# One operand buffer in rows of 512 columns instead of 544, high and low part side by side, in all phases but the small convolution

## The chip, the core and the metric

The kernel runs on one core of one Trainium2 chip. The metric is the device time of one execution in microseconds. All data are float32 in HBM, and so is the result.

## The reference, cut to what matters

Two blocks work one after the other on x with 256 tokens of width 2048. Nearly all of the arithmetic is products of a 256-token activation with weights of 2048 rows.

```python
def first_block(...):
    h = rms_norm(r, g_mix)
    q, k, v, c_b, c_c, c_x, g_a, g_c = split(h @ w_in)           # 2048 x 10240
    attn = moba_attention(rms_norm(q), rms_norm(k), v)           # 8 heads, causal
    y_attn = attn @ w_attn_out
    y_conv = (c_b * causal_depthwise_conv(c_c * c_x, w_conv)) @ w_conv_out
    r = r + (sigmoid(g_a) * y_attn + sigmoid(g_c) * y_conv) @ w_o
    r = r + square(relu(rms_norm(r, g_mlp) @ w_up)) @ w_down     # 8192 wide
    r = r + sigmoid(rms_norm(r, g_ple) @ w_ple_gate) * (p @ w_ple_proj)

def second_block(...):
    h = concatenate([meta_tokens, x])                            # 16 + 256 tokens
    u = rms_norm(h, norm_mix_pre) @ conv_w_in + conv_b_in        # 2048 x 4096
    u = depthwise_conv_31_taps(u_a * sigmoid(u_g)) + conv_b_dw
    h = h + rms_norm(silu(layer_norm(u)) @ conv_w_out + conv_b_out, norm_mix_post)
    u = rms_norm(h, norm_ffn_pre)
    h = h + rms_norm((silu(u @ w_gate) * (u @ w_up)) @ w_down, norm_ffn_post)   # 5632 wide
    return h[:, 16:]
```

The attention of the second block is in the reference's text, but with one layer only the convolution mixer runs.

## The kernel before

**Split products.** Each float32 operand is split into a high part (rounded to `F32R`) and a low part (the rest). A product of two such operands is three products: high by high, high weight by low activation, low weight by high activation. The fourth is left out. The activation's two parts lie one behind the other in a row of one buffer, so that one matmul of 512 columns multiplies the high weight with both (line 456: `hi` by `both_parts(M, kt)`), and a second one of 256 columns multiplies the low weight with the high part (line 459, or line 465 where the low weights come late). I call the two a pair. A pair covers one inner tile `kt` (128 rows of the inner dimension, 16 of them in 2048) and one output tile `m` (128 output features).

**Two operand buffers.** `A` has 16 rows of 2 * TM = 544 columns of four bytes (line 96), since the small convolution's input has 16 meta tokens ahead of the 256. Everywhere else its high part is columns 0 to 255 and its low part columns 272 to 527, so that `both_parts(A, kt)` reads two runs of 256 columns with a gap of 16, and row `kt` begins 2176 * kt bytes behind A's start. `B` has 16 rows of 2 * T = 512 columns (line 97): the two parts touch, the read is one run of 512 columns, and row `kt` begins 2048 * kt bytes behind B's start. `part(M, ...)` (line 131) and `both_parts` (line 136) give these views.

**Which phase reads which.** `A` feeds qk, v, ga, ccx, cb, gc, w_o, down 0 to 3, conv2 (the small convolution's input product, the only phase with 272 columns, lines 745 to 747), out2, and glu 0 to 2 (the gate and up projections of the second block). `B` feeds attn_out, conv_out, up 0 to 3, gate, and back 0 to 2 (the second block's down projection, where the activation is the stationary operand and 512 weight columns move, lines 831 to 833). In v the activation from `A` is stationary too (lines 638 to 640). In out2's and glu 0's first steps two output panels go side by side (lines 495 and 497).

**Weights.** SyncE loads units of 128 x 1024 weights (four inner tiles by two output tiles, 8 pairs) into a ring of four `stage` slots. ScalarE copies each unit to `whi` (line 896), VectorE subtracts to `wlo` (line 1440; GpSimd in conv2, line 2258), TensorE uses the unit. `body` runs two steps, and a step is four units, 32 pairs, into two PSUM banks. While TensorE works on one output panel, ScalarE and VectorE empty the panel before, and where the next phase needs it they write it, split, into the buffer that TensorE isn't reading: into `A` during up, into `B` during glu.

**Order.** All waits are written out by hand with semaphores, one instruction stream per engine; nothing is scheduled by a planner. A unit's wait is at line 440 and following in `step`.

**Grouped steps.** In qk's first two bodies, ga, ccx, and cb's first (`hi_first=True`), and in the first unit of glu 1 and glu 2 (`grouped=0`), the 8 matmuls of 512 columns of a unit run first and its 8 of 256 columns after them (line 465).

Of the kernel before, what the change touches and what calls it, by code (L numbers as in the profile page):

```python
# [32 lines left out]
P = 128  # L33
# [50 lines left out]
def two_block_kernel(nc, io, out):  # L84
    at, _, UNITS = plan()

    with ExitStack() as ctx:
# [346 lines left out]
        def _(pe):  # L434
# [210 lines left out]
            body("qk", 1, A, h1, {2: [lambda: spread(0, xp[:, 0, 0:T], stat_ready)]}, hi_first=True)  # L645
            with pe.Fori(2, 4) as it:
                body("qk", it, A, h1)
            pe.wait_ge(rstd_ready, 1)
# [12 lines left out]
            v_panel(1, {4: [norms(0)]})  # L661
            body("ga", 0, A, h1, beside(0), hi_first=True)
            with pe.Fori(1, 4) as it:
                body("ga", it, A, h1, beside(it), hi_first=True)
            with pe.Fori(0, 3) as it:
                body("ccx", it, A, h1, beside(it + 4), hi_first=True)
            body("ccx", 3, A, h1, beside(7), hi_first=True)
            body("cb", 0, A, h1, beside(8), hi_first=True)
            body("cb", 1, A, h1)
            with pe.Fori(0, 4) as it:  # L670
                body("gc", it, A, h1)

# [14 lines left out]
            with pe.Fori(0, 4) as it:  # L687
                body("w_o", it, A, (merged_ready, 0, 2))

# [31 lines left out]
            ffn_panels("up0", 0, B, (r_ready, 0, 4), first_it=1)  # L721
            ffn_panels("down0", 0, A, (hidden_ready, 0, 2))
# [85 lines left out]
            keep_busy(4, gp[:, 3, :])  # L808
            side_by_side("out2", A, (ln_ready, 0))
            with pe.Fori(1, 4) as it:  # L810
                body("out2", it, A, (ln_ready, 0, 4))
            pe.wait_ge(acc_ready, 36)
# [8 lines left out]
            keep_busy(7, gp[:, 0, :])  # L821
            side_by_side("glu0", A, (r_ready, 48))
            body("glu0", 1, A, (r_ready, 48, 4), {3: [lambda: column_sums(3)]})
# [35 lines left out]
            turn_r(0)  # L859
            body("glu1", 0, A, (r_ready, 48, 4), grouped=0)  # L860
            with pe.Fori(1, 8) as it:
                body("glu1", it, A, (r_ready, 48, 4))
            with pe.Fori(0, 2) as it:
# [3 lines left out]
            turn_r(1)  # L867
            body("glu2", 0, A, (r_ready, 48, 4), grouped=0)
            with pe.Fori(1, 6) as it:
                body("glu2", it, A, (r_ready, 48, 4))  # L870
            for c in range(3):
# [18 lines left out]
        def _(act):  # L890
# [60 lines left out]
            def hi_of_x(c, half):  # L951
                act.wait_ge(x_turned, 2 * c + half + 1)
                for kk in (2 * half, 2 * half + 1):
                    nc.scalar.activation(A[:, 4 * c + kk, 0:T], x_home(c)[:, kk, :], ACT.Copy,
                                         scale=col("g_mix", 4 * c + kk)).then_inc(x_hi, 1)
# [124 lines left out]
            def conv_out_tail(hp, j):  # L1080
                for back in (1, 0) if j == 3 else (1,) if j else ():
                    act.wait_ge(merged, hp - back + 1)
                    nc.scalar.activation(part(A, 0, 2 * (hp - back), 2), s[:, (j - back) % 2, :, 0:T],
                                         ACT.Copy).then_inc(merged_hi, 1)
# [199 lines left out]
            for kt in range(2):  # L1284
                act.wait_ge(ln_normed, kt + 1)
                silu(kt, xp[:, kt, 0:T])
                act.wait_ge(ln_silu, kt + 1)
                nc.scalar.activation(part(A, 0, kt, 1), xp[:, kt, 0:T].unsqueeze(1), ACT.Copy).then_inc(ln_hi, 1)
            for c in range(1, 8):
# [5 lines left out]
                act.wait_ge(ln_silu, 2 * c + 2)  # L1295
                nc.scalar.activation(part(A, 0, 2 * c, 2), ln_home(c), ACT.Copy).then_inc(ln_hi, 2)
                if c == 3:
# [39 lines left out]
            for m in range(2):  # L1337
                act.wait_ge(first_sum, m + 1)
                nc.scalar.activation(part(A, 0, m, 1), r[:, m:m + 1, :], ACT.Copy, scale=col("ffn_pre", m)).then_inc(r_hi, 1)
            for h in range(1, 8):  # L1340
# [6 lines left out]
                act.wait_ge(post_gained, 2 * h)  # L1347
                nc.scalar.activation(part(A, 0, 2 * h, 2), gained_r(h), ACT.Copy).then_inc(r_hi, 2)
                if h == 3:
# [85 lines left out]
        def _(dve):  # L1435
# [100 lines left out]
            for c in range(4):  # L1536
                for kk in range(4):
                    kt = 4 * c + kk
                    if kt == 2:
                        dve.wait_ge(x_turned, 2)  # L1540
                        for i in (2, 3):
                            nc.vector.tensor_scalar(A[:, i, 0:T], x_home(0)[:, i, :], col("g_mix", i), None, ALU.mult).then_inc(first_made, 1)
# [4 lines left out]
                    nc.vector.scalar_tensor_tensor(A[:, kt, TM:TM + T], x_home(c)[:, kk, :], col("g_mix", kt),  # L1547
                                                   A[:, kt, 0:T].bitcast(F32), ALU.mult, ALU.subtract).then_inc(h1_ready, 1)
                take_lo(c, c)
# [172 lines left out]
            def merged_lo(h, j):  # L1722
                dve.wait_ge(merged_hi, h + 1)
                nc.vector.tensor_tensor(part(A, 1, 2 * h, 2), s[:, j, :, 0:T], part(A, 0, 2 * h, 2).bitcast(F32),
                                        ALU.subtract).then_inc(merged_ready, 1)
# [198 lines left out]
            def ln_low(kt, o):  # L1924
                n = o.shape[1]
                dve.wait_ge(ln_hi, kt + n)
                nc.vector.tensor_tensor(part(A, 1, kt, n), o, part(A, 0, kt, n).bitcast(F32), ALU.subtract).then_inc(ln_ready, n)

# [42 lines left out]
            def post_low(h):  # L1971
                dve.wait_ge(r_hi, 48 + 2 * h + 2)
                nc.vector.tensor_tensor(part(A, 1, 2 * h, 2), gained_r(h), part(A, 0, 2 * h, 2).bitcast(F32),
                                        ALU.subtract).then_inc(r_ready, 2)

            def first_low(m):
                dve.wait_ge(r_hi, 48 + m + 1)
                nc.vector.scalar_tensor_tensor(part(A, 1, m, 1), r[:, m:m + 1, :], col("ffn_pre", m),
                                               part(A, 0, m, 1).bitcast(F32), ALU.mult, ALU.subtract).then_inc(r_ready, 1)

# [426 lines left out]
```

## Time and profile before

| what | value |
|---|---|
| device time, median of 3 runs (range) | 2544.76 us (2540.75 to 2545.08) |
| the profiled execution's own time | 2541.44 us |
| its span | 2539.6 us |
| TensorE busy | 2518.6 us, 99% |
| VectorE busy | 1725.2 us, 68% |
| ScalarE busy | 1252.5 us, 49% |
| GpSimd busy | 446.3 us, 18% |
| granted TensorE clock, mean | 0.998 |
| moved by DMA | 466.46 MB, mean 184 GB/s |

The span is the profiled program from its first to its last instruction; the device time of the same execution is 1.84 us longer. Matmuls are pipelined: a row's mean of 393 ns is the time from the start of one matmul to its modelled end, and the next starts before that end. What TensorE really takes is read from start to start.

### The profile page before, as it was taken

The numbers are of one execution on the slowest core, as the hardware profiler recorded it, in microseconds if no ns is written. First come the engines' busy times: TensorE is split into PE (matmuls) and PEld (weight loads), VectorE is DVE, ScalarE is ACT, GpSimd is POOL, SyncE is SP. The second block draws the span as 40 slices with busy tenths as digits, with TensorE's granted clock in tenths as the row PEclk, the third lists the DMA queues.
The fourth block names the chain that finished last, engine by engine and source line by source line (L and its number), as shares of the span: only waits on it lengthen the run. The fifth ranks groups of instructions, "written<-read, shape, count | busy, mean of one in ns | idle before, by whom it ended". The sixth has DMA issues, their size and how long they took to land.

```text
span 2539.6 us, 42560 instructions
## 1 busy us (share of the span) xinstructions
PE 2518.6 (99%) x14597; PEld 2223.8 (88%) x14597; DVE 1725.2 (68%) x2097; ACT 1252.5 (49%) x1554; POOL 446.3 (18%) x303
## 2 busy tenths in 40 slices
PE   9999999999999999999999999999999999999998
PEld 8888888888888888888888899988888888888887
DVE  6568875587765665665667889985766556654665
ACT  6456555554544444444444554555654444444443
POOL 0034410002200000000002378973500000000001
PEclk9999999999999999999999999999999999999999
DMA  7655565665655656556565565536466656656554
GB/s 232 186 168 181 161 189 181 198 192 179 192 188 191 190 186 189 186 191 189 182 197 183 183 173 167 167 109 205 149 192 200 197 181 195 187 192 187 184 183 163
DMA packets 470966, 466.46 MB, mean 184 GB/s; under 512 B 14521, under 2 KB 441011, under 8 KB 470707
## 3 DMA queue, kind: packets, MB, share of 16 engines
q1 hardware_dynamic: 470336, 464.97, 58.6%
q8 instruction: 51, 0.84, 0.1%
q10 hardware_dynamic: 546, 0.38, 0.1%
q14 instruction: 33, 0.27, 0.0%
HBM read 463.20 MB, written 2.10 MB: 183 GB/s over the span
## 4 chain that ended last, share of the span: by engine, by line
PE 87%; DVE 9%; POOL 1%; ACT 1%; issue 1%; DMA 0%; DVEq 0%; POOLq 0%; ACTq 0%; SPq 0%
PE gp L456 48%; PE gp L459 22%; DVE xp L1856 6%; PE gp L832 3%; PE gp L831 3%; PE gp L833 3%; PE gp L465 3%; PE gp L495 1%; PE gp L638 1%; PE gp L639 1%; PE gp L640 1%; DVE wlo L1440 1%; POOL acc L2360 0%; PE xp L792 0%; DVE gp L1821 0%
## 5 line engine op out<-in xcount | busy, mean ns | idle before, releaser
L1440 DVE TENSOR_TENSOR wlo<-stage,whi 128x1024 fp32r<-128x1024 f32 x809 | 1010.0, 1263 | 671.3 <-ACT whi L896 665.9
L896 ACT ACTIVATE whi<-stage 128x1024 fp32r<-128x1024 f32 x874 | 913.5, 1057 | 919.2 <-PE gp L459 591.9
L456 PE MATMUL gp<-A,whi 128*128 128x512 f32 x3968 | 1317.4, 393 | 0.3 <-DVE A L1547 0.3
L459 PE MATMUL gp<-A,wlo 128*128 128x256 f32 x3248 | 911.0, 280 | 0.0
L456 PEld LDWEIGHTS gp<-A,whi 128*128 128x128 f32 x3968 | 738.8, 188 | 161.8 <-DVE A L1547 0.7
L459 PEld LDWEIGHTS gp<-A,wlo 128*128 128x128 f32 x3248 | 612.0, 188 | 0.0
L456 PE MATMUL gp<-B,whi 128*128 128x512 f32 x1536 | 532.9, 391 | 0.5 <-ACT work L1119 0.5
L459 PE MATMUL gp<-B,wlo 128*128 128x256 f32 x1536 | 429.3, 280 | 0.0
L456 PEld LDWEIGHTS gp<-B,whi 128*128 128x128 f32 x1536 | 287.4, 187 | 64.2 <-ACT work L1119 0.7
L459 PEld LDWEIGHTS gp<-B,wlo 128*128 128x128 f32 x1536 | 290.0, 189 | 0.0
L2161 POOL TENSOR_TENSOR sq<-r 128x512 f32 x24 | 29.5, 1227 | 791.1 <-DVE r L1750 755.5
L1856 DVE SCALAR_TENSOR_TENSOR xp<-work,taps,xp 128x256 f32<-128x256 f32 x406 | 162.9, 478 | 1.8 <-PE xp L763 1.8
L2258 POOL TENSOR_TENSOR wlo<-stage,whi 128x1024 fp32r<-128x1024 f32 x64 | 154.4, 2429 | 15.2 <-ACT whi L896 14.9
L745 PE MATMUL gp<-A,whi 128*128 128x272 f32 x512 | 150.6, 294 | 1.1 <-POOL wlo L2258 1.1
L747 PE MATMUL gp<-A,wlo 128*128 128x272 f32 x512 | 147.7, 288 | 0.0
L746 PE MATMUL gp<-A,whi 128*128 128x272 f32 x512 | 147.4, 288 | 0.0
L833 PE MATMUL gp<-whi,B 128*128 128x512 f32 (+1 forms) x352 | 135.3, 384 | 0.0
L832 PE MATMUL gp<-wlo,B 128*128 128x512 f32 (+1 forms) x352 | 135.3, 384 | 0.0
L831 PE MATMUL gp<-whi,B 128*128 128x512 f32 (+1 forms) x352 | 135.2, 384 | 0.0
L2372 POOL TENSOR_TENSOR r<-work 128x1024 f32<-128x1024 f32 (+2 forms) x6 | 10.9, 1810 | 691.1 <-DVE work L2041 684.4
L465 PEld LDWEIGHTS gp<-A,wlo 128*128 128x128 f32 x720 | 96.7, 188 | 8.5 <-DVE wlo L1440 0.4
L909 ACT ACTIVATE cross<-gp 128x512 f32<-128x512 f32 x176 | 102.4, 582 | 3.3 <-PE gp L459 3.3
(333 smaller groups left out, 2171.6 us busy)
## 6 DMA issues: line engine op xcount, KB each, us to landing
stage<-in_w_in SPq DMA_DIRECT2D x160, 512.0 KB, 4.4
stage<-in_w_up SPq DMA_DIRECT2D x128, 512.0 KB, 3.7
stage<-in_w_down SPq DMA_DIRECT2D x128, 512.0 KB, 4.5
stage<-in_ffn_w_gate SPq DMA_DIRECT2D x88, 512.0 KB, 4.5
stage<-in_ffn_w_up SPq DMA_DIRECT2D x88, 512.0 KB, 4.5
stage<-in_ffn_w_down SPq DMA_DIRECT2D x88, 512.0 KB, 4.5
stage<-in_conv_w_in SPq DMA_DIRECT2D x64, 512.0 KB, 4.0
stage<-in_w_o SPq DMA_DIRECT2D x32, 512.0 KB, 4.3
```

The lines of the kernel that those rows point to most:

```text
L456: nc.tensor.matmul(bank.rearrange("p (a t) -> p a t", a=2), hi, both_parts(M, kt), start=first, stop=False)
L459: done = nc.tensor.matmul(bank[:, T:2 * T], lo, M[:, kt, 0:T], start=False, stop=last)
L465: done = nc.tensor.matmul(gp[:, 2 * j + m, T:2 * T], wlo[:, slot, c:c + P], M[:, kt0 + 4 * u + k, 0:T], start=False, stop=u == units - 1 a ...
L745: nc.tensor.matmul(o, hi, A[:, kt, 0:TM], start=first, stop=False)
L747: done = nc.tensor.matmul(o, lo, A[:, kt, 0:TM], start=False, stop=last)
L831: nc.tensor.matmul(o, x_hi, hi[:, c:c + w], start=kt == 0, stop=False)
L832: nc.tensor.matmul(o, x_hi, lo[:, c:c + w], start=False, stop=False)
L833: return nc.tensor.matmul(o, x_lo, hi[:, c:c + w], start=False, stop=last)
L896: nc.scalar.activation(unit_homes(n, slot)[0], stage[:, slot, :], ACT.Copy).then_inc(hi_ready, 1)
L1440: nc.vector.tensor_tensor(lo, stage[:, slot, :], hi.bitcast(F32), ALU.subtract).then_inc(lo_ready, 1)
L1856: nc.vector.scalar_tensor_tensor(dst, x, w, o, ALU.mult, ALU.add).then_inc(tap_done, 1)
L2258: nc.gpsimd.tensor_tensor(wlo[:, slot, :], stage[:, slot, :], whi[:, slot, :].bitcast(F32), ALU.subtract).then_inc(lo_ready, 1)
```

## The change

A view `E` is added on the memory of `A`: its first 16 * 512 columns as 16 rows of 512. Every phase that `A` fed reads and writes `E`, except conv2 and its input, which keep `A` with its rows of 544. Since `E` isn't `A`, `part` puts its low part at column 256, and `both_parts(E, kt)` is one run of 512 columns; row `kt` begins 2048 * kt bytes behind A's start. The buffer's size, all other tensors, and the place and number of the instructions and waits on every engine are as they were. What changes is the addresses, and the shape of line 456's (and 495's) moving operand. `sums_split` for the first two norms still puts its sums in the last row of `A`, and the last two weight units still use A's first 4096 columns (`spare`).

```diff
+        E = A[:].rearrange("p k n -> p (k n)")[:, 0:KT * 2 * T].rearrange("p (k n) -> p k n", k=KT)
...
-            body("qk", 0, A, h1, hi_first=True, mid={c: lambda c=c: turn_x(c + 1) for c in range(3)})
+            body("qk", 0, E, h1, hi_first=True, mid={c: lambda c=c: turn_x(c + 1) for c in range(3)})
...
-                            x_hi, x_lo = A[:, kt, t * P:t * P + P], A[:, kt, TM + t * P:TM + t * P + P]
+                            x_hi, x_lo = E[:, kt, t * P:t * P + P], E[:, kt, T + t * P:T + t * P + P]
...
-                ffn_panels("down0", rnd, A, (hidden_ready, 8 * rnd, 2))
+                ffn_panels("down0", rnd, E, (hidden_ready, 8 * rnd, 2))
...
-            side_by_side("out2", A, (ln_ready, 0))
+            side_by_side("out2", E, (ln_ready, 0))
...
-                body("glu0", it, A, (r_ready, 48, 4))
+                body("glu0", it, E, (r_ready, 48, 4))
...
-                        nc.scalar.activation(part(A, 0, 4 * it + 2 * j, 2), s[:, j, :, 0:T], ACT.Copy).then_inc(up_hi, 1)
+                        nc.scalar.activation(part(E, 0, 4 * it + 2 * j, 2), s[:, j, :, 0:T], ACT.Copy).then_inc(up_hi, 1)
...
-                        nc.vector.tensor_tensor(part(A, 1, 4 * it + 2 * j, 2), t, part(A, 0, 4 * it + 2 * j, 2).bitcast(F32),
+                        nc.vector.tensor_tensor(part(E, 1, 4 * it + 2 * j, 2), t, part(E, 0, 4 * it + 2 * j, 2).bitcast(F32),
                                                 ALU.subtract).then_inc(hidden_ready, 1)
...
```

The other lines of the diff make the same replacement in the phases listed above.

## Rows read from the trace of the kernel before

**Rows 1.** The page: span and busy time of TensorE.
```profile
span 2539.6 us, 42560 instructions
...
PE 2518.6 (99%) x14597; PEld 2223.8 (88%) x14597; DVE 1725.2 (68%) x2097; ACT 1252.5 (49%) x1554; POOL 446.3 (18%) x303
```
**Rows 2.** The page: the chain that ended last, share of the span by engine.
```profile
PE 87%; DVE 9%; POOL 1%; ACT 1%; issue 1%; DMA 0%; DVEq 0%; POOLq 0%; ACTq 0%; SPq 0%
```
**Rows 3.** Busy time by window, down round 0, up round 1 (stretch, length, each engine, PEclk, DMA).
```profile
760.00:849.00 89.00, 89.00 (x513) 78.20 (x513) 50.69 (x51) 38.35 (x41) 0.00 (x0) 1.00 0.60 191
849.00:938.00 89.00, 89.00 (x516) 78.46 (x515) 58.86 (x63) 41.03 (x47) 0.00 (x0) 1.00 0.59 186
```
**Rows 4.** TensorE's instructions by line and form (busy us, mean ns, idle before).
```profile
L456 PE MATMUL gp<-A,whi 128*128 128x512 f32 x3968 | 1317.4, 393 | 0.3 <-DVE A L1547 0.3
L459 PE MATMUL gp<-A,wlo 128*128 128x256 f32 x3248 | 911.0, 280 | 0.0
L456 PE MATMUL gp<-B,whi 128*128 128x512 f32 x1536 | 532.9, 391 | 0.5 <-ACT work L1119 0.5
...
L465 PE MATMUL gp<-A,wlo 128*128 128x256 f32 x720 | 99.0, 280 | 0.0
L495 PE MATMUL gp<-A,whi 128*128 128x512 f32 x128 | 45.9, 401 | 1.2 <-DVE A L1927 1.2
```
**Rows 5.** Timeline, TensorE: first matmul of down 0, up 1, down 1, up 2, down 2.
```profile
760.51 0.39 PE L456 MATMUL gp<-A,whi 128*128 128x512 f32 x1
...
849.68 0.39 PE L456 MATMUL gp<-B,whi 128*128 128x512 f32 x1
...
938.42 0.39 PE L456 MATMUL gp<-A,whi 128*128 128x512 f32 x1
...
1027.60 0.39 PE L456 MATMUL gp<-B,whi 128*128 128x512 f32 x1
...
1116.34 0.39 PE L456 MATMUL gp<-A,whi 128*128 128x512 f32 x1
```
**Rows 6.** Timeline, TensorE: starts of the inner tiles 1 to 8, down round 0.
```profile
761.20 0.39 PE L456 MATMUL gp<-A,whi 128*128 128x512 f32 x1
...
761.90 0.39 PE L456 MATMUL gp<-A,whi 128*128 128x512 f32 x1
...
762.59 0.39 PE L456 MATMUL gp<-A,whi 128*128 128x512 f32 x1
...
763.29 0.39 PE L456 MATMUL gp<-A,whi 128*128 128x512 f32 x1
...
763.98 0.39 PE L456 MATMUL gp<-A,whi 128*128 128x512 f32 x1
...
764.68 0.39 PE L456 MATMUL gp<-A,whi 128*128 128x512 f32 x1
...
765.38 0.39 PE L456 MATMUL gp<-A,whi 128*128 128x512 f32 x1
...
766.08 0.39 PE L456 MATMUL gp<-A,whi 128*128 128x512 f32 x1
```
**Rows 7.** Timeline, TensorE: start of inner tile 8, up round 1.
```profile
855.22 0.39 PE L456 MATMUL gp<-B,whi 128*128 128x512 f32 x1
```
**Rows 8.** The chain that ended last: two units of grouped matmuls, four units apart.
```profile
222.20 1.85 PE gp L456 x8
...
233.35 1.85 PE gp L456 x8
```
**Rows 9.** Timeline, TensorE: wide matmuls, 18 apart, in v and in back 0.
```profile
107.26 0.39 PE L638 MATMUL gp<-whi,A 128*128 128x512 f32 x1
...
111.38 0.39 PE L638 MATMUL gp<-whi,A 128*128 128x512 f32 x1
...
1985.16 0.39 PE L831 MATMUL gp<-whi,B 128*128 128x512 f32 x1
...
1989.24 0.39 PE L831 MATMUL gp<-whi,B 128*128 128x512 f32 x1
```

More of the change, by code:

```diff
@@ L643, in v_panel @@
                         f()
-            body("qk", 1, A, h1, {2: [lambda: spread(0, xp[:, 0, 0:T], stat_ready)]}, hi_first=True)
+            body("qk", 1, E, h1, {2: [lambda: spread(0, xp[:, 0, 0:T], stat_ready)]}, hi_first=True)
             with pe.Fori(2, 4) as it:
-                body("qk", it, A, h1)
+                body("qk", it, E, h1)
             pe.wait_ge(rstd_ready, 1)
@@ L661, in _ @@
             v_panel(1, {4: [norms(0)]})
-            body("ga", 0, A, h1, beside(0), hi_first=True)
+            body("ga", 0, E, h1, beside(0), hi_first=True)
             with pe.Fori(1, 4) as it:
-                body("ga", it, A, h1, beside(it), hi_first=True)
+                body("ga", it, E, h1, beside(it), hi_first=True)
             with pe.Fori(0, 3) as it:
[L666 to L669, printed above, removed]
+                body("ccx", it, E, h1, beside(it + 4), hi_first=True)
+            body("ccx", 3, E, h1, beside(7), hi_first=True)
+            body("cb", 0, E, h1, beside(8), hi_first=True)
+            body("cb", 1, E, h1)
             with pe.Fori(0, 4) as it:
-                body("gc", it, A, h1)
+                body("gc", it, E, h1)
             for phase, kt0, ready in (("attn_out", 0, (attn_ready, HEADS, 0)), ("conv_out", CT, (conv1_ready, 0, 4))):
@@ L687, in _ @@
             with pe.Fori(0, 4) as it:
-                body("w_o", it, A, (merged_ready, 0, 2))
+                body("w_o", it, E, (merged_ready, 0, 2))
             pe.wait_ge(meta_step, 2)
@@ L821, in _ @@
             keep_busy(7, gp[:, 0, :])
-            side_by_side("glu0", A, (r_ready, 48))
-            body("glu0", 1, A, (r_ready, 48, 4), {3: [lambda: column_sums(3)]})
+            side_by_side("glu0", E, (r_ready, 48))
+            body("glu0", 1, E, (r_ready, 48, 4), {3: [lambda: column_sums(3)]})
             with pe.Fori(2, 8) as it:
-                body("glu0", it, A, (r_ready, 48, 4))
+                body("glu0", it, E, (r_ready, 48, 4))
             def products(o, n, slot, kt, k, t, a, w, last):
@@ L859, in _ @@
             turn_r(0)
-            body("glu1", 0, A, (r_ready, 48, 4), grouped=0)
+            body("glu1", 0, E, (r_ready, 48, 4), grouped=0)
             with pe.Fori(1, 8) as it:
-                body("glu1", it, A, (r_ready, 48, 4))
+                body("glu1", it, E, (r_ready, 48, 4))
             with pe.Fori(0, 2) as it:
@@ L867, in _ @@
             turn_r(1)
-            body("glu2", 0, A, (r_ready, 48, 4), grouped=0)
+            body("glu2", 0, E, (r_ready, 48, 4), grouped=0)
             with pe.Fori(1, 6) as it:
-                body("glu2", it, A, (r_ready, 48, 4))
+                body("glu2", it, E, (r_ready, 48, 4))
             for c in range(3):
@@ L1082, in conv_out_tail @@
                     act.wait_ge(merged, hp - back + 1)
-                    nc.scalar.activation(part(A, 0, 2 * (hp - back), 2), s[:, (j - back) % 2, :, 0:T],
+                    nc.scalar.activation(part(E, 0, 2 * (hp - back), 2), s[:, (j - back) % 2, :, 0:T],
                                          ACT.Copy).then_inc(merged_hi, 1)
@@ L1287, in _ @@
                 act.wait_ge(ln_silu, kt + 1)
-                nc.scalar.activation(part(A, 0, kt, 1), xp[:, kt, 0:T].unsqueeze(1), ACT.Copy).then_inc(ln_hi, 1)
+                nc.scalar.activation(part(E, 0, kt, 1), xp[:, kt, 0:T].unsqueeze(1), ACT.Copy).then_inc(ln_hi, 1)
             for c in range(1, 8):
@@ L1295, in _ @@
                 act.wait_ge(ln_silu, 2 * c + 2)
-                nc.scalar.activation(part(A, 0, 2 * c, 2), ln_home(c), ACT.Copy).then_inc(ln_hi, 2)
+                nc.scalar.activation(part(E, 0, 2 * c, 2), ln_home(c), ACT.Copy).then_inc(ln_hi, 2)
                 if c == 3:
@@ L1338, in _ @@
                 act.wait_ge(first_sum, m + 1)
-                nc.scalar.activation(part(A, 0, m, 1), r[:, m:m + 1, :], ACT.Copy, scale=col("ffn_pre", m)).then_inc(r_hi, 1)
+                nc.scalar.activation(part(E, 0, m, 1), r[:, m:m + 1, :], ACT.Copy, scale=col("ffn_pre", m)).then_inc(r_hi, 1)
             for h in range(1, 8):
@@ L1347, in _ @@
                 act.wait_ge(post_gained, 2 * h)
-                nc.scalar.activation(part(A, 0, 2 * h, 2), gained_r(h), ACT.Copy).then_inc(r_hi, 2)
+                nc.scalar.activation(part(E, 0, 2 * h, 2), gained_r(h), ACT.Copy).then_inc(r_hi, 2)
                 if h == 3:
@@ L1546, in _ @@
                         dve.wait_ge(x_hi, 2 if c == 0 else 4 * c + 2 * (kk // 2))
[L1547 to L1548 removed]
+                    nc.vector.scalar_tensor_tensor(E[:, kt, T:2 * T], x_home(c)[:, kk, :], col("g_mix", kt),
+                                                   E[:, kt, 0:T].bitcast(F32), ALU.mult, ALU.subtract).then_inc(h1_ready, 1)
                 take_lo(c, c)
@@ L1723, in merged_lo @@
                 dve.wait_ge(merged_hi, h + 1)
-                nc.vector.tensor_tensor(part(A, 1, 2 * h, 2), s[:, j, :, 0:T], part(A, 0, 2 * h, 2).bitcast(F32),
+                nc.vector.tensor_tensor(part(E, 1, 2 * h, 2), s[:, j, :, 0:T], part(E, 0, 2 * h, 2).bitcast(F32),
                                         ALU.subtract).then_inc(merged_ready, 1)
@@ L1926, in ln_low @@
                 dve.wait_ge(ln_hi, kt + n)
-                nc.vector.tensor_tensor(part(A, 1, kt, n), o, part(A, 0, kt, n).bitcast(F32), ALU.subtract).then_inc(ln_ready, n)
+                nc.vector.tensor_tensor(part(E, 1, kt, n), o, part(E, 0, kt, n).bitcast(F32), ALU.subtract).then_inc(ln_ready, n)
             ln_scale(0, 1)
@@ L1972, in post_low @@
                 dve.wait_ge(r_hi, 48 + 2 * h + 2)
-                nc.vector.tensor_tensor(part(A, 1, 2 * h, 2), gained_r(h), part(A, 0, 2 * h, 2).bitcast(F32),
+                nc.vector.tensor_tensor(part(E, 1, 2 * h, 2), gained_r(h), part(E, 0, 2 * h, 2).bitcast(F32),
                                         ALU.subtract).then_inc(r_ready, 2)
@@ L1977, in first_low @@
                 dve.wait_ge(r_hi, 48 + m + 1)
-                nc.vector.scalar_tensor_tensor(part(A, 1, m, 1), r[:, m:m + 1, :], col("ffn_pre", m),
-                                               part(A, 0, m, 1).bitcast(F32), ALU.mult, ALU.subtract).then_inc(r_ready, 1)
+                nc.vector.scalar_tensor_tensor(part(E, 1, m, 1), r[:, m:m + 1, :], col("ffn_pre", m),
+                                               part(E, 0, m, 1).bitcast(F32), ALU.mult, ALU.subtract).then_inc(r_ready, 1)
             def first_add(m):
```

8 lines of the change are left out of this document (4 added, 4 removed).

## The prediction

> **What bounds the kernel now.** I read the page first: TensorE is busy for 2518.6 of 2539.6 us [rows 1]. Busy does not yet mean that it sets the end, so the chain that ended last comes next: 87% of it is TensorE's own instructions, one behind the other, 9% VectorE's, nearly all of it the taps of the small convolution [rows 2]. Then the stages: in a down round and in the up round behind it TensorE is busy in all 89.00 us, VectorE in 50.69 and 58.86, ScalarE in 38.35 and 41.03, the DMA engines for 0.60 and 0.59 of the time, at a granted clock of 1.00, which is the upper level, 2.4 GHz [rows 3]. So outside the small convolution time is what a matmul takes from start to start, and a nanosecond on each pair counts 4096 times.
>
> **The change, part by part.** No instruction is added, removed or moved on any engine. What changes is where 4096 matmuls of 512 columns find their moving operand (3968 of line 456 and 128 of line 495 [rows 4]): rows start at multiples of 2048 instead of 2176 bytes, and the two runs of 256 columns become one of 512. The mean durations do not price this, 393 ns with A against 391 with B [rows 4], since they run on past the next start. The starts do.
>
> *Ungrouped pairs.* Down and up have the same work: 8 steps of 32 pairs, 256 pairs, weights from the same ring, the same two waits in `step`. Down reads A, up reads B. From the first matmul of a phase to the first of the next [rows 5]: down 0 takes 849.68 - 760.51 = 89.17 us, up 1 takes 938.42 - 849.68 = 88.74, down 1 89.18, up 2 88.74. The difference is 0.44 us for 256 pairs, 1.72 ns a pair: 348.4 ns with A against 346.6 with B. It repeats to 0.01 us, although VectorE and ScalarE have more to do in the up rounds, where TensorE is the quicker [rows 3]. So it is not other engines' work that holds TensorE in down.
>
> Is it the layout? Within A the inner tiles differ, and that is the strongest sign. The eight tiles from 760.51 to 766.08 take in turn 0.69, 0.70, 0.69, 0.70, 0.70, 0.69 ... [rows 5, 6]; summed over the four even tiles (0, 2, 4, 6) 0.69 + 0.69 + 0.69 + 0.70 = 2.77 us, over the four odd ones 4 x 0.70 = 2.80. In B eight tiles take 855.22 - 849.68 = 5.54 us, 2.77 for four [rows 5, 7]. A's even tiles start at multiples of 4352 bytes and run at B's pace; the odd ones start 2176 bytes further and cost 0.03 us more for 8 pairs, some 3.4 ns a pair when fitted to the 1.72 on average. All of E's rows start as B's do (if the tensors lie in the order in which they are declared, B begins 34816 = 17 x 2048 bytes behind A). And E's moving operand is one run of 512, as B's. Both of what could make the difference goes, so I need not know which it is. Term: 3376 ungrouped pairs (4096 less 720) x 1.72 ns = 5.8 us.
>
> *Grouped pairs.* Lines 456 and 465 in units where all 8 wide matmuls run first, 720 pairs in 90 units [rows 4]. No B phase is grouped, so B's pace there is not shown. Four such units take 233.35 - 222.20 = 11.15 us, 2.79 a unit, 348.4 ns a pair [rows 8], the very pace of the ungrouped ones with A. Lower bound: nothing is gained, 0. Upper bound: the 8 wide matmuls, which take 1.85 us now [rows 8], come down to the pace of wide matmuls in a row in back 0, (1989.24 - 1985.16) / 18 = 226.7 ns [rows 9]: 8 x 226.7 = 1.81 us, 0.04 a unit, 3.3 us for all. I take the row that it is nearest to, the 1.72 ns of a pair with the same operands: 1.2 us.
>
> *Stationary operand in v.* Here A's columns are loaded as weights and 512 weight columns move, 192 matmuls, 228.9 ns each (4.12 us / 18); back 0 does the same from B in 226.7 [rows 9]. Bounds 0 and 192 x 2.2 = 0.4 us; I take 0.4, since the form is the same.
>
> *What writes E.* ScalarE and VectorE write the same number of elements in runs of 256 as before. I cost this at nothing: VectorE, the busier of the two, has 30 to 38 us of slack in an up or down round [rows 3]. If a write cost 50 ns more, there are 8 to 16 a round, under 1 us, and the cover would hold. If TensorE goes faster, what is late next? The unit must come every 2.77 us instead of 2.79, and B's phases get it already. Conv2 keeps its rows and its wait on the taps: 0.
>
> Sum: 5.8 + 1.2 + 0.4 = 7.4 us. Nothing hides it, since what is left in the chain is additive: each phase starts when TensorE has finished the one before. The profiled execution took 2541.44 us (span 2539.6 and 1.84 around it), so it would be 2534.0 (span 2532.2). It lies 3.3 us under the median of the runs shown, 2544.76, whose spread is 4.3 us; against the median the forecast is 2544.76 - 7.4 = 2537.4 us.
>
> **A rule that speaks against it.** The rows say that the place or the break of a row costs 1.72 ns a pair [rows 5, 6]. The Trainium skill ("Advanced Engine Details and Errata", SBUF Cachelines) says that reads which fall on the same 16-byte line get full performance; and "Perfetto Trace Analysis" (Contiguity and DMAs) that contiguity "only matters within an SBUF partition line for DMA transfers". A's row starts are multiples of 16 bytes, and so is its gap; by these pages the two layouts would be read alike, and the change would be worth nothing. The trace does not agree as far as TensorE is concerned, with 89.17 against 88.74 us, so the sum goes by the rows, and the pages' outcome is the first rival.
>
> **The rivals.**
> 1. *The layout costs nothing, and down is slower for another reason,* as where its results go: down's panels are added to the residual, up's are not. Then E is as slow as A, and the time is that of before, 2541.4 by the profiled execution, 2544.8 by the median. Against it: TensorE never waits in either [rows 3], the grouped qk-to-cb phases, with quite other results, have the same 348.4 [rows 8], and the odd tiles are picked out [rows 6]. 15%.
> 2. *It gives more:* the grouped units and v go to the pace of wide matmuls in a row. 5.8 + 3.3 + 0.4 = 9.5 us, time 2535.3. It is within the forecast's range, so I count it there.
> 3. *A new collision, slower.* Now TensorE reads one buffer while ScalarE and VectorE write the other, and both have rows at the same multiple of 2048 bytes: in up (reads B, writes E, 1024 pairs) and in glu (reads E, writes B, 1408 pairs). Before, no phase of pairs had this. Place: these 2432 pairs. Price: if both matmuls of a pair paid what an odd tile's pair pays now, 3.4 ns each, 2432 x 6.8 = 16.5 us, less the 7.4 gained: 9.1 us slower, 2553.9. It decides from 7.4 / 2432 = 3.0 ns a pair. Against it: `stage`, `whi` and `wlo` have slots of 4096 bytes, so their rows also begin together, they are written all the time, and TensorE reads `whi` and `wlo` and B beside these writes at the quicker pace [rows 5]. 4%.
> 4. *The change isn't what it says:* a place that still reads or writes the old columns would give wrong products, not another time. A view that stays in two runs would leave half of the difference open: with the start mended and the break not, anything from 0 to 7.4. B's view is made by the same `both_parts`, so I give it no chance of its own.
>
> **How the numbers follow.** About 0.2% (5.1 us) is what a measurement of this kernel can tell from no change. Forecast and rival 2 have 81%, rival 1 15%, rival 3 4%. A true gain of 7.4 us is 0.29%, only 2.3 us beyond that bound, and the runs of before spread over 4.3 us; so of the 81 I put 69 to faster by over 0.2% and 11 to within, 1 to slower by bad luck. With rival 1 (2 faster, 11 same, 2 slower) and rival 3 (1 same, 3 slower): faster 0.71, same 0.23, slower 0.06. The time is the forecast's, 2537.4. The range: the runs shown less 7.4 lie from 2533.3 to 2537.7; with the upper bounds of grouped units and v (2.1 more) from 2531.2. I take 2531.5 to 2545: the upper end takes in rival 1 by the median and leaves rival 3 out.
>
> **What would show it.** Right: the starts of down 0 and up 1 lie 88.74 us apart, as up's do now, and four odd and four even inner tiles both take 2.77; the grouped units take 2.77; in v the wide matmuls are 226.7 apart; up and back unchanged; conv2 from its first to its last matmul as long as before. Wrong: a down round that still takes 89.17 (rival 1), up above 88.74 or glu above 346.6 ns a pair (rival 3), gaps of TensorE ahead of `step`'s units, filled by VectorE or ScalarE, that were not there before, or a granted clock under 1.00 in a stage that had it.

## The result, and the profile after

| | before | changed |
|---|---|---|
| device time, median of 9 runs each | 2544.13 us | 2565.03 us |
| lowest to highest run | 2540.75 to 2545.08 | 2548.38 to 2566.93 |
| the profiled execution (span) | 2541.44 (2539.6) | 2564.32 (2562.5) |

The ratio is 1.0071, with a 95% interval from 1.0061 to 1.0082. The ratio is estimated from all nine runs of each (their means have 1.0072) and so lies below that of the medians, 1.0082: the changed kernel has seven runs from 2562.8 to 2566.9 and two of 2551.4 and 2548.4. The profile is of one of the seven; neither of the two has one. The kernel is slower by 20.9 us in the median, where 7.4 us less were forecast.

The page of the changed kernel (span, busy time by engine, chain by engine) reads like that of before [rows 1, 2], with 23 us more on TensorE:

```profile
span 2562.5 us, 42560 instructions
...
PE 2541.7 (99%) x14597; PEld 2226.3 (87%) x14597; DVE 1725.0 (67%) x2097; ACT 1252.7 (49%) x1554; POOL 446.0 (17%) x303
...
PE 87%; DVE 9%; ACT 1%; POOL 1%; issue 1%; DMA 0%; DVEq 0%; POOLq 0%; ACTq 0%; SPq 0%
```

Its wide matmuls by form (line 457 is the old 456; a view's tile keeps the name A). The mean is 398 ns for both operands, where it was 393 and 391 [rows 4]. So B's matmuls are slower too, although nothing of theirs was changed:

```profile
L457 PE MATMUL gp<-A,whi 128*128 128x512 f32 x3968 | 1331.4, 398 | 0.3 <-DVE A L1548 0.3
...
L457 PE MATMUL gp<-B,whi 128*128 128x512 f32 x1536 | 541.7, 398 | 0.5 <-ACT work L1120 0.5
```

The timeline's first wide matmul of down 0, up 1, down 1 and up 2, as in [rows 5]:

```profile
766.01 0.40 PE L457 MATMUL gp<-A,whi 128*128 128x512 f32 x1
...
856.46 0.40 PE L457 MATMUL gp<-B,whi 128*128 128x512 f32 x1
...
946.92 0.40 PE L457 MATMUL gp<-A,whi 128*128 128x512 f32 x1
...
1037.37 0.40 PE L457 MATMUL gp<-B,whi 128*128 128x512 f32 x1
```

Down 0 takes 856.46 - 766.01 = 90.45 us, up 1 946.92 - 856.46 = 90.46, down 1 90.45, where it was 89.17, 88.74 and 89.18. That is 353.3 ns a pair with E and with B, against 348.3 and 346.7. No other engine has more to do than before [rows 3], and TensorE does not wait (busy by window, 766 to 856 and 856 to 946):

```profile
766.00:856.00 90.00, 90.00 (x511) 78.08 (x510) 50.69 (x50) 38.36 (x41) 0.00 (x0) 1.00 0.60 188
856.00:946.00 90.00, 90.00 (x511) 78.12 (x510) 58.18 (x63) 41.02 (x47) 0.00 (x0) 1.00 0.58 182
```

In the whole trace TensorE's first matmul of conv2 (line 746, was 745) comes 15.7 us later (1488.9 against 1473.2), and from there to the end it is 7.2 us more. Source view of that line, changed kernel and then the kernel before; the phase itself lasts as long as before, 202.7 us from first to last start:

```profile
L746 PE MATMUL gp<-A,whi x512: 284/287/479, 1488.9 to 1691.6; 128*128 128x272 f32 x171
```

```profile
L745 PE MATMUL gp<-A,whi x512: 284/287/479, 1473.2 to 1675.9; 128*128 128x272 f32 x171
```

Two smaller terms of the prediction. Wide matmuls of v, 18 apart (as in [rows 9]): 4.08 / 18 = 226.7 ns, as forecast. Before, the prediction's 18 matmuls gave 228.9; taken over 96 in a row in the same trace it is 229.4, so the gain over v's 192 matmuls is 0.5 us and not 0.4. Grouped units in the chain, four apart (as in [rows 8]): 11.17 us, against 11.15 before; nothing was gained there.

```profile
106.87 0.39 PE L639 MATMUL gp<-whi,A 128*128 128x512 f32 x1
...
110.95 0.39 PE L639 MATMUL gp<-whi,A 128*128 128x512 f32 x1
```

```profile
221.33 1.84 PE gp L457 x8
...
232.50 1.84 PE gp L457 x8
```

**The place where the pace changes.** Read on in the changed kernel's gate phase, which reads B: five pairs up to 1410.14 take 1.77 us, 354 ns each. Then the sums' matmul comes (line 524), behind a wait of 0.27 us. Afterwards 32 pairs take 1433.46 - 1422.37 = 11.09 us, 346.6 ns each. It is the same code of `step`, with the same buffers and the same weights' ring, on both sides of one short break:

```profile
1408.37 0.40 PE L457 MATMUL gp<-B,whi 128*128 128x512 f32 x1
...
1410.14 0.40 PE L457 MATMUL gp<-B,whi 128*128 128x512 f32 x1
...
1410.93 0.39 PE L524 MATMUL xp<-A,ones_r 128*128 128x256 f32 x1 [0.27 <-POOL A L2177]
...
1422.37 0.39 PE L457 MATMUL gp<-B,whi 128*128 128x512 f32 x1
...
1433.46 0.39 PE L457 MATMUL gp<-B,whi 128*128 128x512 f32 x1
```

In the kernel before, the same sums' matmul comes 11.76 us after gate's first, here 11.75 (1410.93 - 1399.18), since both wait for GpSimd:

```profile
1395.19 0.39 PE L523 MATMUL xp<-A,ones_r 128*128 128x256 f32 x1 [0.50 <-POOL A L2176]
```

So the 32 slow pairs at gate's start cost nothing; the wait behind them is 0.27 us instead of 0.50.

And the trace of before had shown that B's pattern is not one thing. In up 0 (at 740 us) narrow and wide rows alternate, 0.39 / 0.27 / 0.40 / 0.28, in up 1 (at 900 us) each pair reads 0.39 / 0.28:

```profile
739.71 0.39 PE L456 MATMUL gp<-B,whi 128*128 128x512 f32 x1
739.94 0.27 PE L459 MATMUL gp<-B,wlo 128*128 128x256 f32 x1
740.05 0.40 PE L456 MATMUL gp<-B,whi 128*128 128x512 f32 x1
740.28 0.28 PE L459 MATMUL gp<-B,wlo 128*128 128x256 f32 x1
...
900.29 0.39 PE L456 MATMUL gp<-B,whi 128*128 128x512 f32 x1
900.52 0.28 PE L459 MATMUL gp<-B,wlo 128*128 128x256 f32 x1
900.64 0.39 PE L456 MATMUL gp<-B,whi 128*128 128x512 f32 x1
900.87 0.28 PE L459 MATMUL gp<-B,wlo 128*128 128x256 f32 x1
```

Taken to the nanosecond from the same trace, the starts in up 0 follow each other by 231, 112, 233, 117, and again so, a pattern of two pairs; in up 1 by 230, 117, 230, 117, 230, 116, which is one pair repeated (the starts are in whole nanoseconds, and 347, 347, 346 is what 346.67 gives). Both have a mean of 346.7. In the changed kernel it is 241, 120, 236, 113, 233, 117, a pattern of three pairs with a mean of 353.3; and with rows of 544 before, a pattern of four pairs, 229, 117, 230, 116, 233, 118, 231, 119, with a mean of 348.3 (the 348.4 of the prediction). Each pattern repeats to the nanosecond of rounding for hundreds of pairs.

### The profile page after: what moved, and what is told of

The parts are those of the page before. It is cut to its first block, busy times and chain, and to the rows that moved or that the text cites. A ratio compares the mean times of both kernels' runs of the same rounds, so it can differ in the third digit from the quotient of the medians.

```text
span 2562.5 us, 42560 instructions
## 1 busy us (share of the span) xinstructions
PE 2541.7 (99%) x14597; PEld 2226.3 (87%) x14597; DVE 1725.0 (67%) x2097; ACT 1252.7 (49%) x1554; POOL 446.0 (17%) x303
## 4 chain that ended last, share of the span: by engine, by line
PE 87%; DVE 9%; ACT 1%; POOL 1%; issue 1%; DMA 0%; DVEq 0%; POOLq 0%; ACTq 0%; SPq 0%
PE gp L457 49%; PE gp L460 22%; DVE xp L1857 6%; PE gp L832 3%; PE gp L833 3%; PE gp L834 3%; PE gp L466 3%; PE gp L496 1%; PE gp L639 1%; PE gp L641 1%; PE gp L640 1%; DVE wlo L1441 1%; ACT whi L897 0%; PE xp L793 0%; DVE gp L1822 0%
## 5 line engine op out<-in xcount | busy, mean ns | idle before, releaser
L457 PE MATMUL gp<-A,whi 128*128 128x512 f32 x3968 | 1331.4, 398 | 0.3 <-DVE A L1548 0.3
L457 PE MATMUL gp<-B,whi 128*128 128x512 f32 x1536 | 541.7, 398 | 0.5 <-ACT work L1120 0.5
L1451 DVE TENSOR_TENSOR s<-gp,cross 128x512 f32<-128x512 f32 x150 | 102.6, 684 | 1.9 <-ACT cross L910 1.6
```

Of the source, the lines that this page charges most:

```text
L457: nc.tensor.matmul(bank.rearrange("p (a t) -> p a t", a=2), hi, both_parts(M, kt), start=first, stop=False)
```

## The experiments

Theories: *state* (or rhythm): TensorE's stream of pairs settles into one of several repeating patterns; which of them are possible depends on where the operands start, which of them comes is decided where the stream starts again after a break, and it is then carried from phase to phase. *Collision* (the prediction's rival 3): reads of rows of 2048 bytes meet writes of the other buffer. *Layout:* each buffer has a pace of its own. "Pace" below is the mean start-to-start time of a pair, worked out from all starts of a phase in the profiled run (behind a wait, without the first 32 pairs). The three steady values of interest are 346.7 (quick), 348.3 (rows of 544) and 353.3 (slow).

### Only down reads E

```diff
-            ffn_panels("down0", 0, A, (hidden_ready, 0, 2))
+            ffn_panels("down0", 0, E, (hidden_ready, 0, 2))
...
-                ffn_panels("down0", rnd, A, (hidden_ready, 8 * rnd, 2))
+                ffn_panels("down0", rnd, E, (hidden_ready, 8 * rnd, 2))
```

(and the two writes of up's result; all else is the kernel before)

> Only down 0 to 3 read rows of 512 (view E), and up writes them; all other phases are those of the kernel before. Rhythm theory: TensorE's pairs fall into a repeating pattern; rows of 544 force one of 348.4 ns a pair, aligned rows allow two, 346.7 or 353, the choice is made where the stream restarts after a wait and is carried over every phase until a 544 phase or a wait. Up 0 starts behind the same wait as before, in the quick pattern, and nothing throws it out: up and down all at 88.7 us, total 4 x 0.44 = 1.8 us under before, about 2542.4. Collision theory (my rival 3): up reads B while E is written, so up takes 90.3 instead of 88.7, down (E read, B not written) 88.7: total +6.4 - 1.8 = +4.6, about 2549. If reading E is slow by itself: down 90.3, up 88.7, +4.7.

Five runs: 2539.09, 2540.47, 2552.83, 2553.40, 2554.49; nothing between. The profile is of the 2539.09 run. Its timeline (first wide matmul of down 0, up 1, down 1) has 88.75 and 88.75:

```profile
759.85 0.39 PE L457 MATMUL gp<-A,whi 128*128 128x512 f32 x1
...
848.60 0.39 PE L457 MATMUL gp<-B,whi 128*128 128x512 f32 x1
...
937.35 0.39 PE L457 MATMUL gp<-A,whi 128*128 128x512 f32 x1
```

So E and B both run at 346.7, in all eight phases, with E being written during up: neither E itself nor the writes cost anything in this run. The gap between the two groups is 13.8 us (means 2539.8 and 2553.6). The eight phases, 2048 pairs, at 6.67 ns more make 13.7. That the upper group is this is an inference from the size; only one run, of the lower group, was profiled. The median forecast of 2542.4 missed that the choice at up 0's start differs from run to run.

### Only the first phases and w_o use rows of 512

The changed kernel with `E` put back to `A` in down, out2 and glu and in the writes for them.

> Only x's split, qk to gc and w_o use rows of 512; down, out2 and glu keep rows of 544. Rhythm theory: qk to gc in the slow pattern (353), attn_out and conv_out inherit it (90.3 us for both instead of 88.6), w_o too, and up 0 as far as it inherits (90.3); down 0 with rows of 544 at 89.17 throws it out, up 1 to 3 again 88.74. Total about +4 to +7 us. Collision theory: attn_out 44.3, conv_out slow, up 0 to 3 all 88.74, w_o quick. Reading-E theory: attn_out, conv_out, up all as before, only qk to gc and w_o slow.

Median 2548.44 of 10 runs (2546.99 to 2549.55), ratio 1.0020 (1.0010 to 1.0029). The pace is 353.3 in gc, and in attn_out and conv_out, which read the untouched B, and in w_o. Up 0, behind a break, came in at 346.7 (I had expected 353.3). Down 0 and up 1, both as before, first wide matmuls of down 0, up 1, down 1:

```profile
764.85 0.39 PE L457 MATMUL gp<-A,whi 128*128 128x512 f32 x1
...
854.02 0.39 PE L457 MATMUL gp<-B,whi 128*128 128x512 f32 x1
...
942.77 0.39 PE L457 MATMUL gp<-A,whi 128*128 128x512 f32 x1
```

89.17 and 88.75, as in [rows 5]. Collision would have spared attn_out, and layout attn_out and conv_out; both fall for these two phases. Gate, at 346.7 as it begins, goes to 353.3 behind its sums' break: the opposite of the changed kernel, in the same code.

### Rows of 544, but no gap

```diff
-        E = A[:].rearrange("p k n -> p (k n)")[:, 0:KT * 2 * T].rearrange("p (k n) -> p k n", k=KT)
+        E = A[:, :, 0:2 * T]
```

> As the changed kernel, but rows start every 544 columns again and only the gap of 16 between high and low part is gone. If the rows' starts make the pattern: 348.4 ns a pair in all A phases, 346.7 in B phases, 2544. If the gap made it: as the changed kernel, 353 ns in both, about 2565. In v 228.9 ns (starts) or 226.7 (gap).

Median 2553.55 of 5 runs (2552.24 to 2556.14), ratio 1.0040 (1.0026 to 1.0054). Neither of the two outcomes. First wide matmuls of down 0, up 1, down 1: 89.60 and 90.46:

```profile
764.57 0.40 PE L457 MATMUL gp<-A,whi 128*128 128x512 f32 x1
...
854.17 0.40 PE L457 MATMUL gp<-B,whi 128*128 128x512 f32 x1
...
944.63 0.40 PE L457 MATMUL gp<-A,whi 128*128 128x512 f32 x1
```

The A phases are at 350.0, steadily, and hand B the slow pattern each time; v came to neither of the two values, with 230.5 ns (over 96 matmuls) where it was 229.4 before and 226.7 in the changed kernel. So the row starts keep the stream from settling at 353.3 in A phases, and the gap is worth another 1.7 ns. What matters more: without the gap the rows of 544 no longer hand on the quick pattern but the slow one.

### High and low parts in two blocks

The high parts in 16 rows of 256 columns, the low parts in 16 more behind them: row starts of 1024 bytes, and the wide matmul's operand in two far runs.

> The high parts of all 16 tiles in one block of 16 x 256 columns, the low parts in a second one behind it: rows start every 1024 bytes, and the wide matmul's operand is again two runs of 256, far apart. If the starts make the pattern: as the changed kernel, 353 ns a pair where it falls into the slow pattern, about 2550 to 2565, and B phases slow with it. If the gap made it: 348.4 and 2544.

Median 2556.99 of 6 runs (2549.02 to 2566.82), ratio 1.0051 (1.0029 to 1.0072). The profiled run (2566.01) has 353.3 in every phase, B's too, gate included, but glu 0's first 160 pairs: they are at 346.7 on both sides of the sums' matmuls, and go to 353.3 at a short gap behind the 160th (565 ns from start to start, where other pairs have 347). The same two patterns as one run of 512: two runs instead of one is not what separates them.

### Down 0 in rows of 544, down 1 to 3 in rows of 512

> Only down 1 to 3 use rows of 512; down 0 keeps rows of 544 and so does all the rest. Rhythm theory: whatever pattern up 0 starts in, down 0's rows of 544 end it and hand the quick one on, so up 1 to 3 and down 1 to 3 all run at 346.7 in every run, there are no slow runs as with only down changed, and the time is 3 x 0.44 = 1.3 us under before, about 2542.4, in one narrow cluster. If the choice were made anew at each phase instead of carried, some runs would be at 2548 to 2554.

Ten runs from 2538.91 to 2541.40, median 2540.62, beside 2541.02 for the kernel before on the same chip: ratio 0.9995 (0.9986 to 1.0005), no change. The two groups of runs are gone. In the profile up 1 to down 3 are all at 346.7. The six phases behind down 0 are all in the quick pattern, as the state theory has it. That one phase in rows of 544 with the gap also brings a slow stream to it is an inference: in this profile up 0 was at 346.7 already, and no profile has a slow stream going into such a phase. For it speaks that up 0 starts with the same code as in the kernel with only down changed, whose times had the slow group in three of five runs, and here it shows in none of ten. The gain of 1.3 us is below what this measurement can show.

### An extra matmul ahead of each up and each down

```diff
+                nc.tensor.matmul(xp[:, 3, 0:P], ones_r[:], ones_r[:], start=True, stop=True)
                 ffn_panels("up0", rnd, B, (r_ready, 0, 4))
+                nc.tensor.matmul(xp[:, 3, 0:P], ones_r[:], ones_r[:], start=True, stop=True)
                 ffn_panels("down0", rnd, E, (hidden_ready, 8 * rnd, 2))
```

> The changed kernel with one extra matmul of 128 columns (ones by ones into a free PSUM bank) ahead of each up and each down phase of rounds 1 to 3, six in all, under 0.6 us together. Rhythm theory: the pattern is a state that an extra instruction can tip, so the pace changes between 353.3 and 346.7 exactly at one or more of the six places (and is carried on from there), and a total of 2550 to 2565 comes out, with times other than the changed kernel's two clusters. If the pace belongs to the layout or to what other engines write, all up and down phases stay at 353.3 and the time is 2565.6.

Median 2559.84 of 4 runs (2556.86 to 2561.95). Up 1, 2 and 3 are at 346.7, down 1, 2 and 3 at 353.3: the pace changes at all six places. It alternates, which state explains by six flips, but layout as well by "B quick, E slow behind such a matmul".

### The extra matmul ahead of up only

> The changed kernel with the extra matmul of 128 columns ahead of up 1, 2 and 3 only, and none ahead of down. In the run with six extra matmuls every up was quick and every down slow, which has two readings. State theory: each extra matmul moves the stream from one pattern to the other (or leaves it), and the pattern is then carried; up 1 and down 1 then have the same pace, 346.7 if up 0 was slow, and up 2 with down 2 either the same or the other. Layout theory: behind an extra matmul B runs quick and E slow, whatever came before; then up 1 to 3 take 88.7 us and down 1 to 3 90.3.

Median 2557.79 of 4 runs (2555.72 to 2559.56). The timeline at the extra matmul ahead of up 1 (line 725), then the starts of down 1, up 2 and down 2:

```profile
857.28 0.22 PE L725 MATMUL xp<-ones_r 128*128 128x128 f32 x1
857.34 0.45 PE L457 MATMUL gp<-B,whi 128*128 128x512 f32 x1
...
946.14 0.39 PE L457 MATMUL gp<-A,whi 128*128 128x512 f32 x1
...
1034.95 0.45 PE L457 MATMUL gp<-B,whi 128*128 128x512 f32 x1
...
1125.45 0.40 PE L457 MATMUL gp<-A,whi 128*128 128x512 f32 x1
```

Up 1 takes 946.14 - 857.34 = 88.80 us, down 1 1034.95 - 946.14 = 88.81 (the next extra matmul in it), up 2 1125.45 - 1034.95 = 90.50. Down 2 is at 353.3 too, and up 3 and down 3 at 346.7 again. B has both paces and E has both paces, in one run, and each change between up 0 and down 3 stands at an extra matmul. That is the state theory's outcome, and layout is out.

### One extra matmul, within up 0

> The changed kernel with a single extra matmul of 128 columns, inside up 0, between its second and third panel. State theory: up 0's first 64 pairs keep their pace, and from the extra matmul on the pace is 346.7 for the other 192 pairs of up 0 and all of down 0 to down 3, 1984 pairs x 6.7 = 13.2 us under the changed kernel's upper cluster, about 2552. Layout theory: the pace of each phase is that of the changed kernel, and the time 2565.

Seven runs: 2550.65, 2551.48, 2551.64, 2551.74 and 2553.67, and 2566.82 and 2566.91. In the profiled run (2553.67) 32 pairs ahead of the extra matmul (line 722) take 698.55 - 687.24 = 11.31 us, 353.4 each, and 32 pairs behind it, 710.11 to 721.20, 11.09, 346.6 each:

```profile
687.24 0.40 PE L457 MATMUL gp<-B,whi 128*128 128x512 f32 x1
...
698.55 0.40 PE L457 MATMUL gp<-B,whi 128*128 128x512 f32 x1
698.79 0.28 PE L460 MATMUL gp<-B,wlo 128*128 128x256 f32 x1
698.90 0.22 PE L722 MATMUL xp<-ones_r 128*128 128x128 f32 x1
...
710.11 0.39 PE L457 MATMUL gp<-B,whi 128*128 128x512 f32 x1
...
721.20 0.39 PE L457 MATMUL gp<-B,whi 128*128 128x512 f32 x1
```

The instruction costs 0.06 us (the next wide matmul starts at 698.96) and the pairs go on at 346.7 through all of down 0 to down 3, and for 1984 pairs that is 13.2 us. Two of seven runs did not get it; that up 0 came in quick there and was tipped to the slow pattern would fit, but those runs have no profile.

### The weights' place

128 bytes left free ahead of `wlo`, and in a second kernel ahead of `whi` (both then move against E and B); the tensors declared behind move as well.

> The changed kernel with 128 bytes left free between whi and wlo, so wlo and all tensors declared after it lie 128 bytes further. Theory a: the pattern arises between TensorE's reads of weights and its reads of the moving operand; then moving wlo against E and B gives another pattern than 346.7 or 353.3 in A and B phases, as A's odd tiles did. Theory b: only the moving operand's own row starts count, from one tile to the next; then it is as the changed kernel, 346.7 or 353.3 a pair and 2548 to 2567.

> The same with the 128 bytes ahead of whi, so that whi and wlo both move against E and B but not against each other. Theory a: again another pattern, since both weight reads move against the moving operand; if only the place of whi to wlo counts, as the changed kernel. Theory b: as the changed kernel, 2548 to 2567.

With only `wlo` moved: the pace is 346.7 in nearly all phases of A and B, 350.0 in w_o, at the end of gate and in glu 0 up to its sums; 353.3 is gone. That is one run, of 2543.91; the ten fall into two groups, 2543.5 to 2545.7 and 2549.8 to 2551.7, and none of the upper one has a profile (2000 pairs at 350.0 instead of 346.7 would make the 6.6 us between them). With both moved: 351.1 in every phase of both buffers, no second value, and four runs within 1.4 us. Theory b is out, since the moving operand's own rows are where they were. What was moved is the weights' place against everything declared ahead of them; that their place against the moving operand says which patterns there are, theory a, is the plain reading, but their place against `stage`, which the DMA fills meanwhile, moved with it and was not tested by itself. Neither is a better kernel: medians 2547.73 of 10 (ratio 1.0028, 1.0018 to 1.0037) and 2563.79 of 4 (1.0090, 1.0073 to 1.0107). The moved tensors made other matmuls slower: in v 231.1 and 232.4 ns instead of 226.7, in back 231.1 and 232.4 instead of 226.7, a grouped unit 2.81 us in both instead of 2.79, and with `wlo` moved alone 1.0 ns more on each of conv2's 1536.

### Rows of 512 in the second block only

> Rows of 512 in out2 and glu 0 to 2 only; the first block is that of the kernel before. State theory: all up and down phases as before (88.7 and 89.2 us), out2 and the glu phases each choose where their stream restarts, as in the changed kernel, and mostly fall into 353.3: 1664 pairs less the grouped ones, about 4.9 ns each, +8 us, 2549 to 2552, with single phases at 346.7 in some runs. If the slow pattern in the changed kernel's second block was handed down from its first block, it is gone here: glu at 346.7 and 2540.

Median 2548.49 of 8 runs (2547.28 to 2550.09), ratio 1.0028 (1.0017 to 1.0039). The first block is as before in every phase, out2 and glu 0 to 2 are at 353.3 from their start. This slow pattern isn't handed down: it is chosen there.

### A version meant to beat both

The changed kernel, down 0 in rows of 544, and the extra matmul early in seven stretches.

> A version meant to beat both: the changed kernel, with down 0 kept in rows of 544 (which always hands on the quick pattern) and one extra matmul of 128 columns early in qk, cb, w_o, out2, glu 0 (behind its norm's sums), glu 1 and glu 2, the stretches that started in the slow pattern in every profile with rows of 512. State theory: each stretch flips to 346.7 at its extra matmul. Against the kernel before: some 2900 pairs x 1.7 = -4.9 us, v -0.5, the slow starts of the stretches (some 200 pairs x 4.9) +1.0, grouped units +0.5, seven extra matmuls +1.0: about 3 us under before. If a stretch enters in the quick pattern, its extra matmul makes it slow, and that costs up to 3.4 us for each stretch of 512 pairs. If the pattern could not be steered, all these stretches stay at 353.3: +12 us or more.

Median 2543.74 of 11 runs, the kernel before 2542.24: ratio 1.0005 (0.9996 to 1.0014). The extra matmul took cb, glu 0, glu 1 and glu 2 from 353.3 to 346.7, as meant. In qk and w_o the pace was 353.3 on both sides of it. Out2 had come in quick, and it made it slow. Glu 0 fell back to 353.3 behind its 160th pair, at the same short gap as with two blocks. In all, it can be steered in four places of seven, and it isn't a better kernel.

The starts to the nanosecond show what the two failures have in common. In all runs together the extra matmul came into a stream at 353.3 in twelve places, where pairs take 361, 349 and 350 ns in turn. In the ten where the pace changed, the pair just ahead of it had begun 348 to 351 ns before; in the two where it stayed, qk and w_o, 361 ns before, so there it followed the pattern's long pair. The five places entered at 346.7 all went to 353.3. No run tested this by moving the extra matmul by one pair, but it says where to put it next.

| pace, ns a pair | gc | attn_out, conv_out | w_o | up 0 | down 0 | up 1 | down 1 | end of gate | glu 1, 2 |
|---|---|---|---|---|---|---|---|---|---|
| before | 348.3 | 346.7 | 348.3 | 346.7 | 348.3 | 346.7 | 348.3 | 346.7 | 348.3 |
| changed | 353.3 | 353.3 | 353.3 | 353.3 | 353.3 | 353.3 | 353.3 | 346.7 | 353.3 |
| down on E | 348.3 | 346.7 | 348.3 | 346.7 | 346.7 | 346.7 | 346.7 | 346.7 | 348.3 |
| first phases on E | 353.3 | 353.3 | 353.3 | 346.7 | 348.3 | 346.7 | 348.3 | 353.3 | 348.3 |
| 544, no gap | 350.0 | 353.3 | 350.0 | 353.3 | 350.0 | 353.3 | 350.0 | 353.3 | 350.0 |
| extra matmul ahead of up | 353.3 | 353.3 | 353.3 | 353.3 | 353.3 | 346.7 | 346.7 | 346.7 | 353.3 |
| `whi` and `wlo` moved | 351.1 | 351.1 | 351.1 | 351.1 | 351.1 | 351.1 | 351.1 | 351.1 | 351.1 |

## Why the prediction was wrong

*What held.* TensorE's start-to-start time sets the end, and next to nothing hides a change of it (gate's first 32 pairs, ahead of the wait for GpSimd, are such a place). The differences that I read were real: 89.17 against 88.74 us, and odd tiles dearer than even ones. V came down to 226.7 ns a matmul, worth 0.5 us, where 0.4 had been forecast. Conv2, the clock and the other engines stayed as they were. In the profiled run even that E would run at B's pace came true, but at a new pace of B.

*The step that failed* is in the part on ungrouped pairs: "Both of what could make the difference goes, so I need not know which it is." I took 346.7 ns for a property of B's layout. It is one of at least two states of a stream that reads aligned rows, and in the kernel before B was in it because each A phase, with rows of 544 and a gap, handed it on (up 1 to 3 behind such phases are at 346.7 in every profile that has them, and with down 0 alone in such rows the slow group of runs is gone). With those rows gone, the stream can stay in the 353.3 pattern from one break to the next, and in the profiled run it does from qk to gate. The term should have been, for that run: from qk to down 3, 1728 ungrouped pairs on E x 5.0 ns = 8.6 us and 1280 on B x 6.67 = 8.5, together 17.2. At conv2's start 15.7 are measured: v gave 0.5 back, and qk's first half, which waits for x, took 1.0 less in this run (its first 32 pairs alone differ by up to 0.7 us between profiles of kernels that are the same up to there). For out2 and glu, 1648 pairs x 5.0 = 8.2, against 7.2; breaks that became shorter took up most of the rest, 0.3 us at glu 0's sums and 0.3 between out2 and glu 0. The sum that I made, 5.8 us for 3376 pairs, had the wrong sign for E and left out B's pairs altogether.

*Grouped pairs:* 1.2 us were forecast, from "the row that it is nearest to"; 0 came, the lower bound.

*The rivals.* The first one (nothing changes) is out: pace does depend on where operands lie, as the 350.0, 351.1 and 346.7 of the moved layouts show. So the pages that the prediction weighed (the Trainium skill, "Advanced Engine Details and Errata", SBUF Cachelines, and "Perfetto Trace Analysis", Contiguity and DMAs) do not cover TensorE's stream here: all starts in these kernels are multiples of 16 bytes, and the pace still ranged over 6.7 ns. Rival 3 had the right sign and a wrong mechanism: writes of E in up cost nothing in the profiled run with down alone on E, and attn_out, with no write to the other buffer, slowed as much as the rest. None of the rivals was a state that is carried. I asked for each edit what it costs, and not what the old layout did for its neighbours. That the times of a deterministic instruction stream fall into groups (2548.4 and 2551.4 against 2562.8 to 2566.9) is what such a state would look like from outside; no program has a profile of both its groups.

*What stays open.* Why the patterns have these lengths. If two accesses within TensorE's stream get in each other's way, no run says which two. The runs say that the weights' place and the moving operand's both bear on it, and no more. Also open is what decides the choice at a break: up 0 in the kernel with down alone on E, by the times, came out both ways in five runs of one program, while glu 1 and 2 started slow in every profile that had them in rows of 512 and the weights in their old place.

## What to carry to other kernels

Where one engine's stream sets the end, read its start-to-start times to the nanosecond and look for the repeating pattern, before taking a phase's pace as the property of its operands. If two phases have different paces, ask what each hands to the next, and test it by changing one phase only. Before aligning a buffer for 1.7 ns, look at the spread over runs afterwards: groups of times can mean that the gain is a state, which neither alignment nor a lucky profile secures.

## What the runs showed of the hardware that I had not expected

All at the granted clock of 1.00, with float32r operands and a pair of 512 and 256 columns with its own weights each.

- The same pair has at least five steady means, 346.7, 348.3, 350.0, 351.1 and 353.3 ns, each from a pattern that repeats and holds for hundreds of pairs: after one or two pairs at 346.7, two or four at 350.0, three at 351.1 and 353.3, four at 348.3. Between 346.7, 348.3, 350.0 and 353.3 lie steps of 1.67 and 3.3, that is 6.7 ns once in four pairs, in two, or in every one; 351.1 would be two in three.
- The pattern survives the change of the operand buffer, of the PSUM bank and of the loop. A single matmul of 128 columns, 0.06 us, changed it in 15 of the 17 places where one was put in a profiled run, in both directions, and not in the two where it followed the long pair of the 353.3 pattern; a wait of 0.27 us with two matmuls did so in gate.
- Wide matmuls in a row (three products with the activation stationary) take 226.7 ns from start to start where the stationary rows start at multiples of 1024 or 2048 bytes, 229.4 at multiples of 2176 with the gap of 64 bytes and 230.5 without it. Weights moved by 128 bytes made it 231.1 or 232.4 with the rows of 2048.
